# The entry of stage 3 begun ahead of the engines' meeting, with the gate row sent through DRAM and the backward states placed among the last taps

## The chip, the cores and the metric

The kernel runs on one core of one Trainium2 chip. The metric is the device time of one launch in microseconds; three runs of a kernel are taken and their median is compared. Beside them one execution is taken by the hardware profiler, and the rows below come from it. A core has TensorE (PE, with its weight loads PEld), VectorE (DVE), ScalarE (ACT), GpSimd (POOL) and SyncE (SP), which only issues DMAs here, and 16 DMA engines.

## What is computed

One inference step of a hybrid layer, for 256 context tokens and 2048 latent tokens of width 1024:

```
h   = rmsnorm(x) * (1 + scale1) + shift1
q,k,v,r,z,ga,gg = split(h @ w_in)
o   = gla_forward(q,k,v,g_f(z)) + gla_backward(q,k,v,g_b(z))   # chunks of 64, 4 heads
o   = rmsnorm_head(o) * silu(r)
u   = silu(layernorm(depthwise_conv31(ga * sigmoid(gg)) + b))
x   = x + gate1 * (concat(o, u) @ w_out)
h   = rmsnorm(x) * (1 + scale2) + shift2
x   = x + gate2 * expert_choice_moe(h)                         # 16 experts
y   = rmsnorm(x)
scale, shift, gate = silu(cond) @ w_mod + b_mod               # one set per request
```

The outputs are y of both token sets and the final forward and backward states of the context.

## The kernel before, in words

All matrices are kept in fp32; a product is made of three matmuls of split operands (a high and a low part, `three`, lines 1519 to 1521). The high part is a copy by ScalarE, the low part a subtraction on VectorE or GpSimd.

**Stage 2** goes over five blocks of tokens: the prompt (256 tokens), then latent blocks 0 to 3 (512 each), by `stage2(b, nb)` on every engine, b the block and nb the next one. TensorE projects the rows (`proj_half`, `proj_part`), makes the intra-chunk scores and outputs (`scores`, `outputs`), and in blocks 0 to 2 also two columns' worth of w_mod products, `mod_chunk(b, 0)` to `(b, 3)`, before and after `outputs(b, 3)`, which `mod_back` turns into columns and VectorE's `mod_tiles` writes into `mod`. w_mod reaches SBUF in two buffers (`raw`), by `load_mod(b, m)` on SyncE's queue; `load_mod(b, 2)` waits until `mod_chunk(b, 0)` has read its buffer. VectorE makes the depthwise convolution as 124 shifted multiply-adds (`taps(b, first, end)`, line 2258, the accumulator in `acc`), with the forward state recursion (`states`, line 2285) at fixed places between them. Results of a block are parked in DRAM: `park_q`, `park_o` (`store_o`), `park_r` (`store_r`), `park_s` (chunk states) and last `park_c` (the convolution), all by SyncE, in the written order of its `stage2`.

**The meeting.** `stage_end(eng, 1)` drains each engine and lets all wait for all. SyncE first waits until every store of the last block has landed (`stage2_done`). SBUF is laid out anew for stage 3: the weights of w_out (`wo_hl`), `cat` (the concatenation), `S3`, `q`, `r`, the staging buffers `wstage`, and `gt1` lie where stage 2 had its tiles.

**Stage 3** goes over m = 0 (the prompt) and m = 1 to 4 (latent blocks 3 down to 0). For each m the parked data are loaded (`load_c`, `load_qS`, `load_o`, `load_r`), the convolution's mean is taken on TensorE (`conv_mean`) and subtracted by VectorE (`centre`), the backward states are formed by VectorE (`back_states`, line 2305), their contribution is multiplied on TensorE (`inter`, line 1764) and added (`add_inter`), sums of squares (`sums`) give the norms (`stat_roots`, `stat_recips`, `stat_hi`, `spread`), and the output projection follows (`out_half`), a tile of 128 tokens at a time. `inter` has two banks: its third head waits until `add_inter` has taken the first.

Stage 3 begins with a `prologue` on TensorE, ScalarE and VectorE for m = 0, in which also w_out is split into parts (`wo_hi(k)` on ScalarE, `wo_lo(k)` on VectorE, in pairs k per staging buffer), the gate row gate1 is spread over all partitions into `gt1`, the router's weights are scaled (`wrA`), and the router's bias row is formed (`brow_of`). Before the change gt1 is made so: VectorE multiplies the identity by a column of `mod` into `diag`, TensorE multiplies ones by diag, ScalarE copies the four banks. Each engine works through its own instructions in the written order and waits on semaphores.

`mod_d` is a small DRAM tensor by which columns of `mod` are turned into rows: later in stage 3 (m = 2) four of its rows are stored, after it two more, each by a DMA of this form:

```
sp.dma_start(mod_d[i, cnd].rearrange("(k p) -> p k", p=128), cols[:, :, cnd],
             allow_slow_non_contiguous=True).then_inc(e_mod.sem, 16)
```

## Time and profile before

| | us |
|---|---|
| median of three runs | 2610.89 |
| lowest and highest | 2608.91, 2612.08 |
| the profiled execution, its own time | 2607.07 |
| its span, first to last instruction | 2605.0 |
| stage 2, last tap | 799.6 |
| first output matmul of stage 3 | 847.57 |

In the page of the profile TensorE is busy 2388.8 us (92%), VectorE 1653.4 (63%), ScalarE 1189.2 (46%), GpSimd 735.0 (28%). The time from some 1330 us on belongs to the experts. All times in rows are us from the start of the span, durations in a timeline are us; "mean ns" columns are marked as such. A timeline row merges neighbouring instructions of one line (x16 is sixteen of them), and in brackets stands how long the engine was idle before it and what released it. In a chain row stand the start, the time that the piece holds the chain, and the engine and line. The granted TensorE clock is given as a share of the full one, 1.00 or 0.50.

### The profile page before, as it was taken

How to read it: one execution, taken by the hardware profiler on the slowest of the kernel's cores; microseconds unless marked ns; L12 is line 12 of the kernel's file. 1: busy time of each engine (PE TensorE's matmuls, PEld its weight loads, DVE VectorE, ACT ScalarE, POOL GpSimd, SP SyncE). 2: the span in 40 equal slices, each digit the busy share in tenths (PEclk: the TensorE clock that was granted, in tenths of full speed). 3: DMA queues.
4: the chain of work that ended last, by engine and by line, in shares of the span. 5: the costliest groups of instructions: out<-in, count | busy, mean ns of one | idle time of the engine just before them, and what ended most of it. 6: DMA issues, size and time to landing. Idle time of an engine off the chain costs nothing.

```text
span 2605.0 us, 41287 instructions
## 1 busy us (share of the span) xinstructions
PE 2388.8 (92%) x15500; PEld 2138.2 (82%) x15500; DVE 1653.4 (63%) x2793; ACT 1189.2 (46%) x1916; POOL 735.0 (28%) x671
## 2 busy tenths in 40 slices
PE   5879999999995899996569999999999999999994
PEld 1868878787894577875169999999999999999994
DVE  1797969689597554523836656666665666666575
ACT  2646354453422333331145555445555545555563
POOL 1000000000000130110033445554445555444451
PEclk9989999999996899997579999999999999999997
DMA  7885575746536556524255667776667776666885
GB/s 242 322 305 193 175 252 182 262 164 227 189 127 207 166 161 143 166 96 128 70 151 185 180 199 199 199 212 191 188 182 205 199 206 196 188 187 196 280 253 193
DMA packets 287555, 505.73 MB, mean 194 GB/s; under 512 B 32094, under 2 KB 230587, under 8 KB 271578
## 3 DMA queue, kind: packets, MB, share of 16 engines
q1 hardware_dynamic: 248042, 377.93, 44.2%
q0 software_dynamic: 39408, 126.38, 18.7%
q8 instruction: 68, 1.11, 0.2%
q14 instruction: 37, 0.30, 0.0%
HBM read 405.73 MB, written 98.53 MB: 194 GB/s over the span
## 4 chain that ended last, share of the span: by engine, by line
PE 57%; DVE 5%; DMA 3%; ACT 2%; issue 1%; POOL 1%; SPq 0%; DVEq 0%; ACTq 0%; POOLq 0%
PE bank L1519 17%; PE bank L1521 17%; PE bank L1520 17%; PE bank L1764 1%; PE bank L1832 1%; DMA work_out<-park_s 1%; DVE work_exp L2511 1%; DMA out_dram<-work_exp 1%; PE bank L1780 1%; PE bank L1821 1%; DVE work_proj L2258 1%; PE bank L1783 1%; DVE work_out L2305 1%; PE bank L1772 1%; POOL x_rows L1458 0%
## 5 line engine op out<-in xcount | busy, mean ns | idle before, releaser
L1519 PE MATMUL bank<-act_hl_exp,hl_exp 128*128 128x288 f32 x3072 | 913.6, 297 | 37.2 <-POOL act_hl_exp L1437 24.0
L1520 PE MATMUL bank<-act_hl_exp,hl_exp 128*128 128x288 f32 x3072 | 910.2, 296 | 0.0
L1521 PE MATMUL bank<-act_hl_exp,hl_exp 128*128 128x288 f32 x3072 | 908.7, 296 | 0.0
L1519 PEld LDWEIGHTS bank<-act_hl_exp,hl_exp 128*128 128x128 f32 x3072 | 579.8, 189 | 40.6 <-issue 28.9
L1521 PEld LDWEIGHTS bank<-act_hl_exp,hl_exp 128*128 128x128 f32 x3072 | 581.8, 189 | 0.0
L1520 PEld LDWEIGHTS bank<-act_hl_exp,hl_exp 128*128 128x128 f32 x3072 | 580.6, 189 | 0.0
L2629 DVE TENSOR_TENSOR hl_exp<-work_exp,hl_exp 128x1024 fp32r<-128x1024 f32 x192 | 231.7, 1227 | 228.5 <-ACT hl_exp L1126 228.5
L2629 DVE TENSOR_TENSOR hl_exp<-raw_exp,hl_exp 128x1024 fp32r<-128x1024 f32 x192 | 232.2, 1225 | 200.5 <-ACT hl_exp L1126 200.5
L2258 DVE SCALAR_TENSOR_TENSOR work_proj<-work_proj,wcv 128x392 f32<-128x392 f32 (+11 forms) x600 | 337.0, 634 | 0.0
L1126 ACT ACTIVATE hl_exp<-work_exp 128x1024 fp32r<-128x1024 f32 x192 | 199.4, 1055 | 218.5 <-PE bank L1521 213.0
L1126 ACT ACTIVATE hl_exp<-raw_exp 128x1024 fp32r<-128x1024 f32 x192 | 198.5, 1052 | 166.5 <-PE bank L1521 166.4
L1437 POOL TENSOR_TENSOR act_hl_exp<-work_exp,act_hl_exp 128x288 fp32r<-128x288 f32 x128 | 156.3, 1239 | 386.9 <-ACT act_hl_exp L1149 386.9
L1458 POOL DMA_INDIRECT x_rows<-work_exp x135 | 242.9, 1799 | 61.6 <-issue 36.0
L1519 PE MATMUL bank<-act_hl_proj,hl_proj 128*128 128x512 f32 (+1 forms) x672 | 246.8, 367 | 5.8 <-DVE hl_proj L2105 4.2
L1521 PE MATMUL bank<-act_hl_proj,hl_proj 128*128 128x512 f32 (+1 forms) x672 | 242.7, 361 | 0.0
L1520 PE MATMUL bank<-act_hl_proj,hl_proj 128*128 128x512 f32 (+1 forms) x672 | 242.6, 361 | 0.0
L1307 POOL DMA_DIRECT2D hl_proj<-park_w x80 | 42.7, 535 | 645.1 <-PE bank L1521 565.8
L1424 POOL DMA_INDIRECT work_exp<-h_rows,work_exp x135 | 160.6, 1190 | 49.1 <-issue 36.6
L1142 ACT ACTIVATE work_exp<-work_exp 128x256 f32<-128x256 f32 (+1 forms) x256 | 109.4, 497 | 115.3 <-DVE work_exp L2639 67.0
L1519 PEld LDWEIGHTS bank<-act_hl_proj,hl_proj 128*128 128x128 f32 x672 | 128.7, 192 | 26.0 <-issue 5.5
L1521 PEld LDWEIGHTS bank<-act_hl_proj,hl_proj 128*128 128x128 f32 x672 | 128.2, 191 | 19.0
L1520 PEld LDWEIGHTS bank<-act_hl_proj,hl_proj 128*128 128x128 f32 x672 | 128.6, 191 | 17.5
(330 smaller groups left out, 3456.0 us busy)
## 6 DMA issues: line engine op xcount, KB each, us to landing
hl_proj<-park_w POOLq DMA_DIRECT2D x80, 1024.0 KB, 5.5
raw_exp<-in_w_e_gate_dram SPq DMA_DIRECT2D x32, 1024.0 KB, 5.7
raw_exp<-in_w_e_up_dram SPq DMA_DIRECT2D x32, 1024.0 KB, 5.7
work_exp<-in_w_e_gate_dram SPq DMA_DIRECT2D x32, 1024.0 KB
work_exp<-in_w_e_up_dram SPq DMA_DIRECT2D x32, 1024.0 KB, 6.4
raw_exp<-in_w_e_down_dram SPq DMA_DIRECT2D x32, 1024.0 KB, 5.5
work_exp<-in_w_e_down_dram SPq DMA_DIRECT2D x32, 1024.0 KB, 5.5
park_w<-hl_proj SPq DMA_DIRECT2D x10, 2048.0 KB, 11.8
```

The costliest lines, as they stand in the source:

```text
L1126: act.activation(half_out(j, q, 0), half_in(src, j, q), ACT.Copy).then_inc(s_hi, 1)
L1142: last = act.activation(h32e[:, k % 2, a:z], xT[:, k % 2, a:z], ACT.Identity, scale=A2q[:, cnd, k:k + 1], bias=sh2q[:, cnd, k:k + 1])
L1307: pool.dma_start(hl[:, j % 2, q], park_w[j, :, q]).then_inc(s_w[j % 2][q].sem, 16)
L1424: pool.indirect_dma_start(xg[:, b, :], None, h2_rows[:, :], bass.IndirectOffsetOnAxis(ap=ids_g[:, b:b + 1], axis=0)).then_inc(e_gat, 16)
L1437: pool.tensor_tensor(xe_hl[:, 1, k, :], h32e[:, k % 2, :], xe_hl[:, 0, k, :].bitcast(f32), ALU.subtract)\
L1458: pool.indirect_dma_start(x2_quarters[:, :], bass.IndirectOffsetOnAxis(ap=ids_s[:, b:b + 1], axis=0), y_t[:, b, :], None, compute_op=ALU.a ...
L1519: pe.matmul(out, lh, rh, start=first, stop=False)
L1520: pe.matmul(out, lh, rl, start=False, stop=False)
L1521: return pe.matmul(out, ll, rh, start=False, stop=last_)
L1764: last = pe.matmul(psum[7 - h % 2][:, 64 * cc:64 * cc + 64], S3[:, cc + 1, 128 * h:128 * h + 128], part("q", m, h)[:, 64 * cc:64 * cc + 64 ...
L2258: dve.scalar_tensor_tensor(out=ac[:, :, a0:a1], in0=uu[:, :, a0 + off:a1 + off], scalar=wcv[:, ct, w:w + 1], in1=ac[:, :, a0:a1], op0=ALU. ...
L2629: dve.tensor_tensor(half_out(j, q, 1), half_in(src, j, q), half_out(j, q, 0).bitcast(f32), ALU.subtract) .then_inc(s_lo[j % 2], 1)
```

## The change

Parts of stage 3's entry are moved ahead of the meeting. SyncE loads c, q, the states, o and r of m = 0 behind the last `store_o` of the last block; the first three loads of w_out are issued ahead of the drain, behind the landing of park_c. The gate row goes through DRAM: in block 1 (`b.i == 1`), behind `store_r(b, n, 3)` and ahead of `load_mod(b, 2)`, two DMAs store gate1's columns into a fourth row pair of `mod_d`, and behind the meeting two broadcast loads fill `gt1`; diag, its matmuls and the copies are gone, and the first residual waits for the loads. TensorE makes conv_mean(0) and both bias products at the end of its stage 2. VectorE puts `back_states(0, ...)` and `centre(0)` behind the fourth of the last twelve taps. In the prologues, ScalarE's head squares go ahead of wo_hi(2), and wrA goes behind wo_lo(3).

```diff
--- before.py
+++ after.py
@@ -124,7 +124,7 @@
         h2_rows = dram("h2_rows", (NTOK * NQ, HQ))
         h2_of = h2_rows.rearrange("(t q) c -> t q c", q=NQ)
         x2_quarters = x2_rows.rearrange("t (q c) -> (t q) c", q=NQ)
-        mod_d = dram("mod_d", (3, 2, D))
+        mod_d = dram("mod_d", (4, 2, D))
         park_q = dram("park_q", (1 + NBLK, 128, H, BT))
         park_o = dram("park_o", (1 + NBLK, 128, H, BT))
         park_r = dram("park_r", (1 + NBLK, 128, H, BT))
@@ -212,7 +212,6 @@
         selc = W3["selc"].rearrange("p (h c) -> p h c", h=5)
         spread_rs = reset.bitcast(f32r)[0:64, 0:BT]
         spread_sel = reset.bitcast(f32r)[0:64, BT:BT + 5]
-        diag = W3["sq"].rearrange("p (j c) -> p j c", j=16)
         wstage = [W3[n].rearrange("p (k c) -> p k c", k=2) for n in ("x", "xn", "h2")]
 
         def part(name, m, h):
@@ -339,7 +338,7 @@
 
         r_qS, r_o, r_r, r_c = sem("r_qS"), sem("r_o"), sem("r_r"), sem("r_c")
         r_wh, r_wl = sem("r_wh"), sem("r_wl")
-        r_sel, r_dg, r_gt, r_gr = sem("r_sel"), sem("r_dg"), sem("r_gt"), sem("r_gr")
+        r_sel, r_gst, r_gr = sem("r_sel"), sem("r_gst"), sem("r_gr")
         r_wr, r_br = sem("r_wr"), sem("r_br")
         r_c0, r_bs, r_c1, r_nst = sem("r_c0"), sem("r_bs"), sem("r_c1"), sem("r_nst")
         r_in, r_o1, r_sq, r_me, r_xc, r_csq = (sem("r_in"), sem("r_o1"), sem("r_sq"), sem("r_me"), sem("r_xc"),
@@ -541,11 +540,23 @@
                 store_o(b, n, 1 if b.prompt else 2)
                 store_r(b, n, 2)
                 store_r(b, n, 3)
+                if not b.prompt and b.i == 1:
+                    b.wait(sp, s_modv, 0)
+                    for cnd in range(2):
+                        sp.dma_start(mod_d[3, cnd].rearrange("(k p) -> p k", p=128), mod[:, 16:24, cnd],
+                                     allow_slow_non_contiguous=True).then_inc(r_gst, 16)
                 if not b.prompt:
                     if b.mod:
                         load_mod(b, 2)
                         load_mod(b, 3)
                     store_o(b, n, 3)
+                if nb is None:
+                    stage2_done(sp, Blk(b.i - 1))
+                    b.wait(sp, s_qst, 16)
+                    load_c(0)
+                    load_qS(0)
+                    load_o(0)
+                    load_r(0)
                 b.wait(sp, s_fs, b.NC)
                 b.wait(sp, s_ue, b.NC)
                 sp.dma_start(park_s[n, :, 0:b.NC, :], S_t[:, 0:b.NC, :]).then_inc(s_sst.sem, 16)
@@ -631,15 +642,14 @@
                 stage2(Blk(i), Blk(i + 1))
             stage2(final, None)
             stage2_done(sp, final)
+            final.wait(sp, s_c1, 1)
+            wo_v = w_out[0].rearrange("(j k p) c -> j p k c", p=128, k=2)
+            for i in range(3):
+                sp.dma_start(wstage[i], wo_v[i]).then_inc(r_wo[i].sem, 16)
             stage_end(sp, 1)
-            wo_v = w_out[0].rearrange("(j k p) c -> j p k c", p=128, k=2)
-            load_c(0)
-            load_qS(0)
-            load_o(0)
-            sp.dma_start(wstage[0], wo_v[0]).then_inc(r_wo[0].sem, 16)
-            load_r(0)
-            sp.dma_start(wstage[1], wo_v[1]).then_inc(r_wo[1].sem, 16)
-            sp.dma_start(wstage[2], wo_v[2]).then_inc(r_wo[2].sem, 16)
+            sp.wait_ge(r_gst, 32)
+            for cnd in range(2):
+                sp.dma_start(gt1[:, cnd, :], mod_d[3, cnd].partition_broadcast(128)).then_inc(r_gr, 16)
             sp.wait_ge(r_bs, NC3[0])
             sp.dma_start(new_bwd[0, 0].rearrange("h k v -> k h v"),
                          S3[64:128, 0, :].rearrange("k (h v) -> k h v", h=H)).then_inc(r_nst, 16)
@@ -975,8 +985,6 @@
                     act.wait_ge(r_xc, 4 * m + ct + 1)
                     if ct == 0:
                         wait_pos(act, r_st, m)
-                        if m == 0:
-                            act.wait_ge(r_gt, 4)
                     act.activation(part("sq", m, ct), cat_f(m)[:, 4 + ct, :], ACT.Square).then_inc(r_csq, 1)
 
             def head_squares(m, heads=range(H)):
@@ -1048,13 +1056,9 @@
                 conv_squares(0)
                 wo_hi(0)
                 wo_hi(1)
-                for j in range(4):
-                    act.wait_ge(r_gt, j + 1)
-                    act.activation(gt1[:, j // 2, 512 * (j % 2):512 * (j % 2) + 512], psum[j][:, :], ACT.Copy)\
-                       .then_inc(r_gr, 1)
+                head_squares(0)
                 wo_hi(2)
                 wo_hi(3)
-                head_squares(0)
                 wo_hi(4)
                 wo_hi(5)
                 stat_roots(0)
@@ -1692,6 +1696,12 @@
                     mod_chunk(b, 2)
                     mod_chunk(b, 3)
                     mod_back(b)
+                if nb is None:
+                    conv_mean(0)
+                    b.wait(pe, s_ue, b.NC)
+                    b.wait(pe, s_modv, 0)
+                    brow_of(0)
+                    brow_of(1).then_inc(r_br, 1)
 
             def mod_chunk(b, m):
 
@@ -1804,7 +1814,6 @@
                         wait_pos(pe, r_lg, g - 2 if late(g - 2) else g - 1)
                 elif q == 0:
                     pe.wait_ge(r_wl, KC)
-                    pe.wait_ge(r_gr, 4)
                 for k in range(KC):
                     if q == 0 and k % 4 == 0:
                         upto(pe, r_lo, piece(m, t, k // 4))
@@ -1833,26 +1842,16 @@
                                      stop=(k == KC - 1))
                 last.then_inc(r_ro, 1)
 
+            def brow_of(c):
+                for k in range(KC):
+                    last = pe.matmul(psum[5][:, NE * c:NE * c + NE], mod[:, 24 + k, c:c + 1].broadcast_to([128, 128]),
+                                     wr[:, k, :], start=(k == 0), stop=(k == KC - 1))
+                return last
+
             def prologue():
-                def brow_of(c):
-                    for k in range(KC):
-                        last = pe.matmul(psum[5][:, NE * c:NE * c + NE],
-                                         mod[:, 24 + k, c:c + 1].broadcast_to([128, 128]), wr[:, k, :],
-                                         start=(k == 0), stop=(k == KC - 1))
-                    return last
-
-                conv_mean(0)
-                for j in range(16):
-                    pe.wait_ge(r_dg, j + 1)
-                    last = pe.matmul(psum[j // 4][:, 128 * (j % 4):128 * (j % 4) + 128], ones[:, :], diag[:, j, :],
-                                     start=True, stop=True)
-                    if j % 4 == 3:
-                        last.then_inc(r_gt, 1)
                 inter(0)
-                brow_of(0)
                 pe.wait_ge(r_sel, 7)
                 sums(0)
-                brow_of(1).then_inc(r_br, 1)
                 spread(0)
                 pe.wait_ge(r_wr, 2)
 
@@ -2228,7 +2227,11 @@
                     lo_rows(nb, 3)
                 taps(b, 106, 112)
                 states(b, 3)
-                taps(b, 112, TAPS)
+                taps(b, 112, 116)
+                if nb is None:
+                    back_states(0, 0, NC3[0])
+                    centre(0)
+                taps(b, 116, TAPS)
 
             def glu(b, ct):
                 b.wait(dve, s_sg, ct + 1)
@@ -2361,6 +2364,8 @@
                 for q in range(2):
                     upto(dve, r_T, 2 * g + q + 1)
                     if q == 0:
+                        if g == 0:
+                            dve.wait_ge(r_gr, 32)
                         upto(dve, r_x[g % 2], 16 * (g // 2 + 1))
                         wait_pos(dve, r_h2st[g % 2], 16 * (g // 2))
                         if g >= 2:
@@ -2382,25 +2387,20 @@
 
             def prologue():
                 dve.tensor_tensor(spread_sel, ident[0:64, 0:5], ident[0:64, 32:37], ALU.add)
-                for j in range(16):
-                    dve.tensor_scalar(diag[:, j, :], ident[:, :], mod[:, 16 + j % 8, j // 8:j // 8 + 1], None, ALU.mult)\
-                       .then_inc(r_dg, 1)
-                for c in range(2):
-                    dve.tensor_tensor(wrA[:, c], wr[:, :, :], A2[:, :, c:c + 1].broadcast_to([128, KC, NE]),
-                                      ALU.mult).then_inc(r_wr, 1)
 
                 def wo_lo(k):
                     dve.wait_ge(r_wh, k + 1)
                     dve.tensor_tensor(wo_hl[:, 1, k, :], wstage[k // 2 % 3][:, k % 2, :], wo_hl[:, 0, k, :].bitcast(f32),
                                       ALU.subtract).then_inc(r_wl, 1)
 
-                centre(0)
-                back_states(0, 0, NC3[0])
                 wo_lo(0)
                 wo_lo(1)
                 add_inter(0)
                 wo_lo(2)
                 wo_lo(3)
+                for c in range(2):
+                    dve.tensor_tensor(wrA[:, c], wr[:, :, :], A2[:, :, c:c + 1].broadcast_to([128, KC, NE]),
+                                      ALU.mult).then_inc(r_wr, 1)
                 gate_heads(0)
                 wo_lo(4)
                 wo_lo(5)
```

## Rows read from the trace of the kernel before

**Rows 1.** Windows: busy us per engine, clock, DMA share; a middle block; one later slice

```profile
340.00:497.00 157.00, 155.88 (x920) 127.80 (x919) 125.20 (x198) 74.80 (x119) 10.81 (x20) 1.00 0.64 214
852.00:853.00 1.00, 1.00 (x4) 0.81 (x3) 0.00 (x0) 0.00 (x0) 1.00 (x2) 0.58 0.88 295
```

**Rows 2.** Chain of waits over the passage, 799 to 848 us

```profile
799.61 3.83 DMA park_c<-work_proj
...
805.62 10.40 DMA work_out<-park_s
...
821.58 7.06 PE bank L1764 x32
828.64 3.33 PE bank L1839 x16
...
847.57 0.77 PE bank L1519
```

**Rows 3.** Timeline of SyncE's queue, the passage

```profile
789.00 0.53 SPq L511 DMA_DIRECT2D park_o<-work_proj  x1
...
803.66 0.58 SPq L584 DMA_DIRECT2D work_out<-park_c  x1
```

**Rows 4.** Timeline of VectorE, the passage

```profile
792.80 6.77 DVE L2258 SCALAR_TENSOR_TENSOR work_proj<-work_proj,wcv 128x432 f32<-128x432 f32 x12
...
807.38 0.48 DVE L2389 TENSOR_TENSOR work_out<-wr,A 128x128 f32<-128x128 f32 x2
811.53 1.42 DVE L2321 SCALAR_TENSOR_TENSOR work_out<-bank,work_out 128x256 f32<-128x256 f32 x4 [3.66 <-PE bank L1772]
...
816.69 4.74 DVE L2305 SCALAR_TENSOR_TENSOR work_out<-work_out,dec 64x128 f32<-64x128 f32 x16
...
829.01 2.35 DVE L2394 TENSOR_TENSOR wo_hl<-work_out,wo_hl 128x1024 fp32r<-128x1024 f32 x2
831.28 1.43 DVE L2336 TENSOR_TENSOR work_out<-work_out 128x256 f32<-128x256 f32 x4
...
837.95 1.74 DVE L2341 RECIPROCAL work_out<-work_out 5x256 f32<-5x256 f32 x1 [2.97 <-ACT work_out L992]
```

**Rows 5.** Timeline of ScalarE, the passage

```profile
819.93 2.00 ACT L1046 ACTIVATE wo_hl<-work_out 128x1024 fp32r<-128x1024 f32 x2 [3.17 <-DMA work_out<-in_w_out_dram]
...
828.73 1.34 ACT L987 ACTIVATE work_out<-work_out 128x256 f32<-128x256 f32 x4 [2.77 <-PE bank L1764]
```

**Rows 6.** Timeline of SyncE's queue, end of block 1

```profile
466.71 10.23 SPq L506 DMA_DIRECT2D park_r<-work_proj  x2
477.65 3.84 SPq L502 DMA_DIRECT2D raw_proj<-in_w_mod_dram  x2
```

**Rows 7.** Timeline of TensorE, block 1 and the end of block 3

```profile
484.15 7.07 PE L1702 MATMUL bank<-raw_proj,scond 128*2 128x256 f32 x32 [0.35 <-DMA raw_proj<-in_w_mod_dram]
...
786.53 1.16 PE L1748 MATMUL bank<-work_proj 128*128 128x128 f32 x8
```

**Rows 8.** DMA issues: count, KB each, median us to landing; 837 to 853.5 us

```profile
work_out<-park_q SPq DMA_DIRECT2D x1, 1024.0 KB, 5.5
```

**Rows 9.** SyncE's queue around 1003; landings of L616, that store's and all

```profile
1003.14 1.06 SPq L661 DMA_DIRECT2D mod_d<-A  x2
1004.25 2.84 SPq L661 DMA_DIRECT2D mod_d<-mod  x2
1014.18 0.33 SPq L616 DMA_DIRECT2D x_rows<-work_out  x1
...
DMA to landing us min/median/max: 10.3/10.3/10.3
...
DMA to landing us min/median/max: 2.6/2.7/17.3
```

**Rows 10.** Timeline of SyncE's queue around 1297

```profile
1297.63 1.00 SPq L703 DMA_DIRECT2D mod_d<-mod  x2
1301.08 0.56 SPq L682 DMA_DIRECT2D raw_exp<-in_w_e_gate_dram  x1
```

**Rows 11.** DMA issues, 1297 to 1312 us

```profile
raw_exp<-in_w_e_gate_dram SPq DMA_DIRECT2D x1, 1024.0 KB, 16.4
```

## The prediction

> **What bounds the kernel now.** I read the table of windows first. In a middle block of stage 2 TensorE is busy 155.88 of 157 us and VectorE 125.20 [rows 1]: until the last block ends, whatever makes TensorE late is paid in full, and there is no slack behind in which to make it up. Then comes the chain of waits over the passage from stage 2 to stage 3 [rows 2]. The last tap ends at 799.6, the store of park_c takes 3.83 us, the engines meet, the loads go out, the later half of the states lands at 805.62 + 10.40 = 816.02, the backward states run until 821.4, inter(0) takes 7.06 us at the low clock, the first bias product 3.33, then come the sums, the roots, the reciprocal at 837.95, and the first output matmul at 847.57. That is 48 us with TensorE mostly idle or waiting, and it is what the change attacks. The timeline of SyncE's own queue comes third [rows 3], because the change issues DMAs in three places of it, one of them two blocks earlier.
>
> **Entry loads and VectorE.** The six loads for m = 0 go out behind the last store_o, issued at 789.00 [rows 3], so from about 789.9. Before, the first was issued at 803.66 [rows 3] and the states were there at 816.02 [rows 2], 12.4 us later, with 0.5 MB each of c, q and twice S ahead and w_out interleaved behind. The new order has the same 2 MB ahead and park_s (2 MB) behind in place of w_out, so I keep 12.4 us: the states land at 802.3. The inserted work stands behind tap 115. States(3) end at 792.8, twelve taps take 6.77 [rows 4], 0.56 each, so tap 115 ends at 795.1 and VectorE then waits 7.2 us for the load, with eight taps queued behind the wait, and behind those the park_c store and the meeting. Backward states with their memset: 816.02 to 821.44, 5.4 us [rows 2] (16 products 4.74 [rows 4]) until 807.7. Centring 1.42 [rows 4] until 809.1 (its conv_mean runs on an idle TensorE). Eight taps, 4.5, until 813.6. park_c 3.83 [rows 2] until 817.4. So VectorE leaves stage 2 14 us later than before, and 5.4 + 1.4 of that is work that only changed sides; the rest is the wait.
>
> **Behind the meeting.** The first w_out pair needs SBUF that park_c's source holds, so it is issued at 817.6. A 1 MB load with others close behind it landed in 5.5 us (park_q, [rows 8]), so call T = 823.1 the time that w_out's first pair is there. inter(0) begins at the meeting, near 818, but its third head needs the bank that add_inter frees, and add_inter stands behind wo_lo(0) and wo_lo(1), so T sets the pace. Two wo_hi of 1.0 [rows 5], one wo_lo of 1.2 [rows 4], one addition (about 0.4, estimated from the centring's 1.42 for four of that size), two heads of inter at 7.06/4 each [rows 2]: T + 7.1 = 830.2. Head squares 1.34 [rows 5]: 831.5, and only then wo_hi(2) and (3), 2.0, for which wo_lo(3) waits: 834.7. wrA 0.48 for both, gate_heads 1.43, wo_lo(4) and (5) 2.35 [rows 4]: the reciprocal starts at 839.0, before at 837.95 [rows 4]. From there the chain to the first output matmul is unchanged (9.6 us). Balance of the passage: **+1 us**. What is taken out there buys nothing: diag (VectorE waits afterwards anyway), the gate matmuls and the four copies of gt1, and brow 3.33 on the chain [rows 2], whose time is given back because the wo_hi/wo_lo pairs, formerly done before TensorE got there, now start at T. Moved into TensorE's idle end of stage 2, conv_mean and both brows cost nothing; without that cover they would cost about 3.5 us each. The two gt1 broadcasts have until the first residual, tens of us. Bounds: if the states arrive at 798 (2 MB at nearly the full rate), 4.3 us less, -3.3 in all; if w_out's first pair shares the queue evenly with the second and third and needs 10 us, +5.5. How much longer than an instant the drain takes with loads under way no row shows; a meeting as late as the end of the w_out loads lies inside the upper bound. I take +1.
>
> **The gate row's way out, in block 1.** Each of the two stores to mod_d writes 1024 elements of 4 bytes, one per packet. They are issued behind store_r(3), that is at 466.71 + 10.23 = 476.9, and straight behind them load_mod(2), before issued at 477.65 [rows 6]. It landed at 484.15, which is where TensorE began mod_chunk(2), having waited 0.35 us for that very DMA [rows 7]: no slack at all. What do such stores do to the queue? The trace has them twice, same shape and same queue. Four of them went out from 1003.14; the x2_rows store issued at 1014.18 landed after 10.3 us [rows 9], against 2.7 as the median of that line [rows 9], so the queue was blocked until about 1021.8, 18.7 us for four, 9.3 for two. Two of them went out at 1297.63, and the weight load issued at 1301.08 [rows 10] landed 16.4 us later [rows 11], 19.9 us after the first store (here gathers shared the engines). Carried to block 1: by the first, 476.9 + 9.3 + 6.5 (the load's own 477.65 to 484.15) = 492.7, TensorE late by 8.6; by the second, 476.9 + 19.9 = 496.8, late by 12.7. I take 10.5, between them, a little nearer the one without gathers. load_mod(3), the park_o and park_s stores and the x tiles follow in the queue; none is due sooner than the delay allows. The array goes cold in such a wait: after the idle passage the dense output matmuls started at 847.57 [rows 2] and ran at the low clock until the slice 852 to 853, where the grant is 0.58 in the mean [rows 1]; 5 us at half speed cost 2.5. Together **+13 us**, and since TensorE is the bound there [rows 1], all of it reaches the end.
>
> The queue model behind this has a page. The trace shows a read delayed by stores that stand ahead of it in the same queue [rows 9, 11]. "DMA: Bandwidth & Descriptors" of the Trainium skill, section Queues, rings and completion order, says that on each DMA engine a ring's descriptors are consumed in order, and its Rules for kernel authors that a strided last dimension becomes one descriptor per element; so far the trace agrees. But the same page, section Two DMAs through the same engine are not ordered, says that descriptors are pipelined and a later one need not wait for an earlier one's write. By that alone the load would go once the small packets are read; the rows say longer. It is rival A, priced below from rows.
>
> **Sum.** 13 + 1 = +14 us. The profiled execution took 2607.07 us (span 2605.0), 3.8 below the median of the three runs: 2621 in an execution like it, 2625 as the median. Own range 2618 (8.6 + 2 of block 1, -3.3 of the passage) to 2632 (12.7 + 2.5 and +5.5).
>
> **Rivals.**
> A. The load passes the stores' slow writes and is late only by half of the smaller figure, 4.3 us, too short for the clock to fall far. For it: in block 1 nobody needs the stores' landing. Against: the 10.3 and 16.4 us. 4.3 + 1 gives 2616.
> B. The stores are hidden altogether: the queue takes them while load_mod(2) is still waiting for mod_chunk(0), and nothing is late. Then only +1 is left, 2612, no measurable change; the change then moves work that was hidden, and its saving is nil. Against it: 0.35 us of wait shows no slack.
> C. Faster: the states land before tap 115 ends, since nothing but park_o is under way at 789.9. The 7.2 us wait vanishes: passage 1 - 7.2 = -6.2, 2605 if block 1 loses nothing. It is a gain that a measurement can tell only if the states land by 796 (6 us after issue, half of what the trace shows) and block 1 is late by less than 1 us. This is what the change would give if the early loads were as free as they look.
>
> **How the numbers follow.** Forecast 0.52, A 0.14, B 0.22, C 0.12. About 0.2% (5 us) is what a measurement can tell from no change. Slower by more: the forecast and most of A, 0.63. Within: B and the rest of A, 0.25. Faster: 0.12. The range runs from 2608 (B with the passage at its lower bound) to 2632; C and the tails are left out, under 2 in 10.
>
> **What would show it.** In block 1 a wait of 8 to 13 us of TensorE for the DMA of w_mod into raw_proj, with the grant at 0.5 behind it, and every later block shifted by 11 to 15 us. In VectorE's last block a wait of about 7 us for park_s after the fourth of the last twelve taps. The meeting some 14 us later against the end of TensorE's stage 2; ACT's first wo_hi some 5 us behind the meeting; the time from TensorE's last product of stage 2 to the first output matmul 60 to 61 us, as before (786.53 + 1.16 = 787.7 [rows 7] to 847.6). The forecast is wrong if the w_mod load lands in its usual 6.5 us, or if that last stretch shrinks by more than 4 us.

## The result and the profile after

The changed kernel takes 2621.9 us, the median of five runs (2620.7 to 2627.6), against 2610.9 for the kernel before (2608.5 to 2612.1): ratio 1.0053, 95% interval [1.0042, 1.0065]. It is slower; the medians differ by 11.0 us, the ratio stands for 13.8 (0.0053 x 2610.9), the forecast was +14. The profiled execution took 2623.2 us, its span is 2621.5.

Block 1 first. SyncE's queue in the changed kernel, start and duration in us, answers to [rows 6]:

```profile
474.34 0.32 SPq L505 DMA_DIRECT2D park_r<-work_proj  x1
474.71 1.45 SPq L546 DMA_DIRECT2D mod_d<-mod  x2
476.20 3.16 SPq L501 DMA_DIRECT2D raw_proj<-in_w_mod_dram  x2
482.83 5.83 SPq L510 DMA_DIRECT2D park_o<-work_proj  x1
```

TensorE in the same block answers to [rows 7]:

```profile
471.72 7.07 PE L1712 MATMUL bank<-raw_proj,scond 128*2 128x256 f32 x32
...
492.17 8.72 PE L1712 MATMUL bank<-raw_proj,scond 128*2 128x256 f32 x32 [10.66 <-DMA raw_proj<-in_w_mod_dram]
```

The same 32 products waited 0.35 us for this DMA before [rows 7] and wait 10.66 now; they take 8.72 instead of 7.07, since the first of them run at the low clock. Together +12.0 us in one place. The windows show the wait from the side of the DMA engines (columns as in [rows 1]: TensorE's busy time first, and last the clock, the DMA engines' busy share, GB/s):

```profile
474.00:482.00 8.00, 7.52 (x47) 4.19 (x44) 8.00 (x13) 2.94 (x6) 0.00 (x0) 1.00 0.74 154
482.00:486.00 4.00, 0.00 (x0) 0.00 (x0) 3.87 (x12) 0.80 (x2) 0.00 (x0) 0.92 0.83 39
486.00:488.00 2.00, 0.00 (x0) 0.00 (x0) 2.00 (x4) 0.00 (x0) 0.00 (x0) 0.50 0.79 39
488.00:490.00 2.00, 0.00 (x0) 0.00 (x0) 2.00 (x5) 0.00 (x0) 0.00 (x0) 0.50 0.72 205
490.00:492.00 2.00, 0.00 (x0) 0.00 (x0) 1.29 (x3) 0.00 (x0) 0.00 (x0) 0.50 1.06 363
492.00:496.00 4.00, 3.83 (x11) 1.17 (x12) 0.00 (x0) 0.00 (x0) 0.00 (x0) 0.55 1.15 406
496.00:500.00 4.00, 4.00 (x20) 1.61 (x19) 0.00 (x0) 0.00 (x0) 0.00 (x0) 1.00 0.96 408
```

From 482 to 488 the DMA engines are four fifths busy and move 39 GB/s; ten microseconds later, at a share of 0.96, they move 408. What they are busy with shows in the packets on record, from 476 to 482 and from 482 to 488:

```profile
DMA packets 2291, 0.63 MB, mean 105 GB/s; under 512 B 2112, under 2 KB 2120, under 8 KB 2248
...
DMA packets 230, 0.24 MB, mean 39 GB/s; under 512 B 0, under 2 KB 230, under 8 KB 230
```

The 4-byte pieces pass in the first six microseconds. In the second six none of them is on record, and the 230 packets have 1 KB each, the size in which w_mod is read: the loads are under way, at a tenth of their later rate. The two stores land only some 12 us after their issue, at about 487, and from 488 on the rate comes back:

```profile
mod_d<-mod SPq DMA_DIRECT2D x2, 4.0 KB, 12.0
```

By this trace the loads pay for the time until the stores have landed, and not only for that in which the pieces go out. TensorE's clock falls to 0.50 (1.2 GHz) in the idle stretch and is back at 1.00 (2.4 GHz) from 496 on.

Then the passage: the chain of waits of the changed kernel, start, time held, engine and line; it answers to [rows 2].

```profile
801.54 10.64 DMA work_out<-park_s
...
823.60 3.83 DMA park_c<-work_proj
827.55 5.02 DMA work_out<-in_w_out_dram
832.59 1.06 ACT wo_hl L1054
...
836.43 3.69 PE bank L1774 x16
840.20 1.33 ACT work_out L995 x4
...
848.89 1.66 DVE work_out L2344
...
858.42 0.77 PE bank L1523
```

VectorE's timeline there answers to [rows 4]:

```profile
802.53 2.38 DVE L2261 SCALAR_TENSOR_TENSOR work_proj<-work_proj,wcv 128x432 f32<-128x432 f32 x4
812.34 0.48 DVE L2300 MEMSET work_out<- 64x512 f32 x1 [7.44 <-DMA work_out<-park_s]
812.86 4.73 DVE L2308 SCALAR_TENSOR_TENSOR work_out<-work_out,dec 64x128 f32<-64x128 f32 x16
...
819.09 4.48 DVE L2261 SCALAR_TENSOR_TENSOR work_proj<-work_proj,wcv 128x416 f32<-128x416 f32 x8
```

VectorE now stands for 7.44 us in front of the states, with eight taps, the store of park_c and the meeting behind it; then the chain runs the same links as before, in another order. The last product of stage 2 is

```profile
796.26 1.16 PE L1758 MATMUL bank<-work_proj 128*128 128x128 f32 x8
```

and ends at 797.42. From there to the first output matmul at 858.42 it is 61.0 us, before 847.57 - 787.69 = 59.9 [rows 2, 7]. So the passage, rebuilt from end to end, is 1.1 us longer than it was, in this pair of executions. That is no more than it varies by itself: in the eight kernels below whose stage 3 is that of before (e2, e3, e5, e6, e9 to e12) it took 59.0 to 61.6 us. What is shown is that it got no shorter.

The two places give 12.0 + 1.1 = 13.1 us. The spans of the profiled executions differ by more, 16.5, because single executions scatter: up to block 1 the changed one was 2.3 us ahead (471.72 against 474.00 at the first w_mod product), and behind the first output matmul it took 2621.5 - 858.4 = 1763.1 us against 1757.4. In the profiles of the six kernels below that have before's stage 3 and ran on chips as fast as these (e2, e3, e5, e6, e11, e12) that rest was 1758.6 to 1766.0. The 1763.1 lies inside, the 1757.4 just below, so no effect of the change shows there.

### The profile page after: what moved, and what is told of

Read it like the earlier page. It is cut to its first block, busy times and chain, and to the rows that moved or that the text cites. A ratio compares the mean times of both kernels' runs of the same rounds, so it can differ in the third digit from the quotient of the medians.

```text
span 2621.5 us, 41212 instructions
## 1 busy us (share of the span) xinstructions
PE 2389.6 (91%) x15468; PEld 2137.2 (82%) x15468; DVE 1651.7 (63%) x2777; ACT 1187.1 (45%) x1912; POOL 734.9 (28%) x671
## 4 chain that ended last, share of the span: by engine, by line
PE 79%; DVE 5%; DMA 5%; ACT 2%; issue 1%; POOL 1%; SPq 1%; ACTq 0%; DVEq 0%; POOLq 0%
PE bank L1523 23%; PE bank L1525 22%; PE bank L1524 22%; PE bank L1774 1%; PE bank L1841 1%; PE bank L1712 1%; DMA raw_proj<-in_w_mod_dram 1%; PE bank L1739 1%; DMA work_out<-park_s 1%; DVE work_exp L2511 1%; PE bank L1751 1%; DMA out_dram<-work_exp 1%; PE bank L1830 1%; PE bank L1758 1%; DVE work_out L2308 1%
## 5 line engine op out<-in xcount | busy, mean ns | idle before, releaser
L1462 POOL DMA_INDIRECT x_rows<-work_exp x135 | 242.8, 1798 | 61.6 <-issue 36.0
```

Source lines behind the costliest of these rows:

```text
L1462: pool.indirect_dma_start(x2_quarters[:, :], bass.IndirectOffsetOnAxis(ap=ids_s[:, b:b + 1], axis=0), y_t[:, b, :], None, compute_op=ALU.a ...
```

## The experiments

In "before plus ..." the kernel before is kept and only the two stores (or a form of them) are put into block 1, into DRAM that nobody reads later; `mod_d` is made larger for them, and SyncE waits for their landing ahead of the meeting. A wait of TensorE is read from one profiled execution per kernel; the same two stores gave 10.66 us in the changed kernel and 9.72 in e2, so differences of 1 us between waits mean nothing. Each comes with runs of before on the same chip; times are compared only there.

### Which of the two places costs the time

**e1_stores_elsewhere**: the whole change, with the two stores moved from block 1 to block 2, behind the store of park_q.

```diff
+                if not b.prompt and b.i == 2:
+                    b.wait(sp, s_modv, 0)
+                    for cnd in range(2):
+                        sp.dma_start(mod_d[3, cnd].rearrange("(k p) -> p k", p=128), mod[:, 16:24, cnd],
+                                     allow_slow_non_contiguous=True).then_inc(r_gst, 16)
                 for j in range(7, NPROJ):
...
                 store_r(b, n, 3)
-                if not b.prompt and b.i == 1:
...
```

> The changed kernel with one edit: the two stores of the gate columns go out in block 2 behind the store of park_q, where the queue has nothing to issue for some 37 us, and not in block 1 ahead of a w_mod load. Queue theory (the small stores hold up the load behind them, TensorE waits 10.7 us for it and then runs 1.65 us longer at the low clock): the wait in block 1 is 0.4 us again, the kernel is about 12 us faster than the changed one, 2610, level with the kernel before within 3 us. Rival (the loss is in the passage to stage 3, the wait of block 1 would be made up later): no change, 2620 to 2622.

Measured: 2608.9 us, before 2609.4, ratio 0.9996 [0.9987, 1.0005]. The same products in block 1:

```profile
483.09 7.07 PE L1712 MATMUL bank<-raw_proj,scond 128*2 128x256 f32 x32 [0.42 <-DMA raw_proj<-in_w_mod_dram]
```

The wait is gone and so is the whole loss. The passage is still 61.2 us long (787.22 to 848.37). At their new place the stores cost nothing that shows: SyncE issues no other DMA for 34 us behind them, and the longest wait of TensorE for a DMA in the rest of that block is 0.7 us.

**e2_stores_alone**: before plus the two stores as the change has them.

```diff
                 store_r(b, n, 3)
+                if not b.prompt and b.i == 1:
+                    b.wait(sp, s_modv, 0)
+                    for cnd in range(2):
+                        sp.dma_start(mod_d[3, cnd].rearrange("(k p) -> p k", p=128), mod[:, 16:24, cnd],
+                                     allow_slow_non_contiguous=True).then_inc(r_gst, 16)
```

> The kernel before with one addition: the same two stores at the place that the change gave them (block 1, ahead of the w_mod load), read by nobody. Queue theory: TensorE waits 10 to 11 us in block 1, the kernel is 11 to 13 us slower than before, 2622 to 2624. Rival (the loss is in the passage): 2611, no change.

Measured: 2620.8 us, before 2609.4, ratio 1.0043 [1.0031, 1.0055], which is +11.2:

```profile
492.14 9.23 PE L1709 MATMUL bank<-raw_proj,scond 128*2 128x256 f32 x32 [9.72 <-DMA raw_proj<-in_w_mod_dram]
```

Two DMAs of 4 KB each, whose result nobody uses, make up the loss. The wait and the time lie a little under what I had expected (10 to 11, 2622). The two runs close the account: the stores cost about 11 us, and all the rest of the change together (e1) nothing that can be told from zero, -3.4 to +1.3 by the interval.

### What it is in the stores

**e3_contiguous_store**: before plus one store of the same 8 KB, left in the order in which it lies in SBUF, so 128 pieces of 64 bytes.

```diff
+                if not b.prompt and b.i == 1:
...
+                    sp.dma_start(mod_d[3].rearrange("c (p e) -> (c p) e", e=16), mod[:, 16:24, :].rearrange("p k c -> p (k c)")).then_inc(r_gst, 16)
```

> The kernel before with the same 8 KB stored at that same place, but in 128 pieces of 64 bytes by one DMA and not in 2048 pieces of 4 bytes by two; read by nobody. If the number of small writes is what holds the queue up: a wait under 1.5 us in block 1 and a time within 2 us of before, 2610 to 2613. If any store to DRAM at that place delays the load by the time of its landing: a wait of some 3 us or more in block 1, 2614 or more. If even 64-byte pieces are as slow as 4-byte ones in sum: 2621 or more.

Measured: 2609.4 us, ratio 1.0001 [0.9993, 1.0010].

```profile
483.58 7.07 PE L1707 MATMUL bank<-raw_proj,scond 128*2 128x256 f32 x32 [0.22 <-DMA raw_proj<-in_w_mod_dram]
```

The same bytes at the same place cost nothing that shows. This is no finished cure: in this order they aren't the row that the broadcast loads read, and no run tested the re-ordering.

**e6_four_stores**: e2 with four such stores instead of two.

```diff
-                    for cnd in range(2):
+                    for r_, cnd in ((3, 0), (3, 1), (4, 0), (4, 1)):
-                        sp.dma_start(mod_d[3, cnd].rearrange("(k p) -> p k", p=128), mod[:, 16:24, cnd],
+                        sp.dma_start(mod_d[r_, cnd].rearrange("(k p) -> p k", p=128), mod[:, 16:24, cnd],
```

> The kernel before with four stores of 4-byte pieces (16 KB in all) and not two, at the place of the change in block 1; read by nobody. If each store adds its own time to the queue (18.7 us for four in the trace of before, so about 4.7 each): a wait of 18 to 20 us in block 1, 2629 to 2632. If most of the two stores' delay is a fixed price of one slow write at the end: a wait of 11 to 13 us, 2621 to 2624.

Measured: 2628.3 us, before 2609.5, ratio 1.0070 [1.0055, 1.0085].

```profile
498.48 8.48 PE L1709 MATMUL bank<-raw_proj,scond 128*2 128x256 f32 x32 [18.03 <-DMA raw_proj<-in_w_mod_dram]
```

Four stores, 18.0 us of wait; two, 9.7. The price of such stores adds up, 4.2 us for each one more; the 18.7 that [rows 9] give for four lie near.

**e9_pieces_apart**: e2 with the same 1024 pieces of 4 bytes in each store, each piece 512 bytes from the next in DRAM.

```diff
+        mod_w = dram("mod_w", (2, D, 128))
...
-                        sp.dma_start(mod_d[3, cnd].rearrange("(k p) -> p k", p=128), mod[:, 16:24, cnd],
+                        sp.dma_start(mod_w[cnd].rearrange("(k p) e -> p k e", p=128)[:, :, 0], mod[:, 16:24, cnd],
```

> The kernel before with the two stores of 1024 pieces of 4 bytes at the place of the change in block 1, but into a DRAM tensor in which the pieces lie 512 bytes apart and not side by side; read by nobody. The pieces, their number and their source are the same. If the price is the number of small pieces: a wait of TensorE of 9 to 12 us for the w_mod load, 2619 to 2623, as with the stores alone (9.7 us, 2620.8). If it is that pieces written side by side by different DMA engines collide in one stretch of DRAM: a wait under 3 us, 2609 to 2612.

Measured: 2636.2 us, before on this chip 2628.4, ratio 1.0033 [1.0022, 1.0044]. (This chip is the slower one for both kernels, and the surplus lies in the experts' part: 1777.7 us behind the first output matmul.) TensorE's wait is 4.64 us:

```profile
486.55 8.41 PE L1710 MATMUL bank<-raw_proj,scond 128*2 128x256 f32 x32 [4.64 <-DMA raw_proj<-in_w_mod_dram]
```

Neither expectation holds: 4.6 us is between the two. About half of the 9.7 us of e2 thus goes with the pieces' lying side by side and not with their count and size. This rests on the waits of two profiled executions, on two chips; in total time the intervals of e2 and e9 overlap.

**e11_wide_pieces_apart** and **e12_wide_pieces_adjacent**: again two stores of 1024 pieces, but each piece 64 bytes wide (data of `wr`), in e11 (below) 512 bytes apart, in e12, where `mod_w` is (2, D, 16), side by side.

```diff
+        mod_w = dram("mod_w", (2, D, 128))
...
+                        sp.dma_start(mod_w[cnd].rearrange("(k p) e -> p k e", p=128)[:, :, 0:NE], wr[:, :, :],
```

> Before with two stores at the change's place in block 1, each of 1024 pieces as in the change, but each piece 64 bytes (16 elements of the router's weights) and the pieces 512 bytes apart in DRAM, into a tensor that nobody reads. Same count of pieces and same spacing as the run with 4-byte pieces apart, where TensorE waited 4.6 us. If it is the count of pieces that holds the DMA engines, the wait stays at 4 to 6 us and the kernel is some 8 us above before. If it is the write of less than 64 bytes, the wait falls to 2 us or less and the time is within 3 us of before.

> The same stores of 1024 pieces of 64 bytes each, with the pieces side by side in DRAM. By the count of pieces alone: as the 4-byte stores side by side, where TensorE waited 9.7 us, or at least as the pieces apart (4 to 6 us). If several pieces that share 64 bytes of memory are what made the stores of the change dear, these, which share none, cost no more than the pieces apart: a wait under 5 us. If short writes as such are the price, a wait of 2 us or less.

Measured: 2612.5 us, ratio 1.0014 [1.0003, 1.0025], and 2613.9 us, ratio 1.0013 [1.0001, 1.0026], before 2609.6. The wait is the same in both:

```profile
483.68 7.07 PE L1710 MATMUL bank<-raw_proj,scond 128*2 128x256 f32 x32 [2.13 <-DMA raw_proj<-in_w_mod_dram]
```

```profile
484.72 7.07 PE L1710 MATMUL bank<-raw_proj,scond 128*2 128x256 f32 x32 [2.13 <-DMA raw_proj<-in_w_mod_dram]
```

Sixteen times the bytes, a fifth of the wait. With 64-byte pieces the distance makes no difference that shows; with 4-byte pieces it halves the wait. As an estimate from single waits, that of e2 falls into about 2.1 us for 2048 pieces as such (e3, with 128, has 0.2), 2.5 for their being 4 bytes and not 64 (4.64 - 2.13), and 5.1 for several of them falling next to each other (9.72 - 4.64). That the last is several short writes to one small stretch of memory, taken one after another, is my reading of it and not shown: no run varied the distance between 4 and 512 bytes, so how far apart is far enough stays open.

### Is it the place in the queue

**e5_stores_by_act**: before plus the two stores issued from ScalarE's queue, behind its `gate(b, 3)`, instead of ahead of the loads in SyncE's.

```diff
                 gate(b, 3)
+                if not b.prompt and b.i == 1:
+                    b.wait(act, s_modv, 0)
+                    for cnd in range(2):
+                        act.dma_start(mod_d[3, cnd].rearrange("(k p) -> p k", p=128), mod[:, 16:24, cnd],
+                                      allow_slow_non_contiguous=True).then_inc(r_gst, 16)
```

> The kernel before with the two 4-byte-piece stores added at the same moment of block 1, but issued from ScalarE's own queue behind the block's last gate, so that they stand in another ring than the w_mod load; read by nobody. If what holds the load up is its place behind the stores in one ring: TensorE's wait in block 1 stays under 3 us, the kernel within 3 us of before, 2609 to 2612. If the small writes block the DMA engines themselves, whatever the ring: a wait of 7 us or more, 2616 to 2621, as with the stores alone on SyncE's queue (9.7 us, 2620.8).

Measured: 2629.3 us, before 2609.5, ratio 1.0071 [1.0059, 1.0084]: worse than in SyncE's queue. ScalarE's queue and TensorE:

```profile
473.67 1.03 ACTq L912 DMA_DIRECT2D mod_d<-mod  x2
```

```profile
500.35 9.00 PE L1709 MATMUL bank<-raw_proj,scond 128*2 128x256 f32 x32 [17.17 <-DMA raw_proj<-in_w_mod_dram]
```

And the landings in that stretch (KB each, median us from issue to landing):

```profile
raw_proj<-in_w_mod_dram SPq DMA_DIRECT2D x2, 1024.0 KB, 23.0
park_r<-work_proj SPq DMA_DIRECT2D x1, 256.0 KB, 21.5
park_o<-work_proj SPq DMA_DIRECT2D x1, 256.0 KB, 17.3
```

In the changed kernel park_r, issued just ahead of the stores in the same queue, landed after 7.5 us and the w_mod loads behind them after 16.6. Here the stores go out first, and every transfer takes turns with them: from 476 to 485, 25 packets of GpSimd's loads are on record and 22 of the stores. And where e2 has one slow stretch, there are two (the last number of a row is GB/s):

```profile
476.00:485.00 9.00, 7.18 (x45) 4.07 (x43) 8.87 (x16) 3.44 (x6) 0.00 (x0) 1.00 0.61 23
485.00:488.00 3.00, 0.00 (x0) 0.00 (x0) 3.00 (x8) 0.00 (x0) 0.00 (x0) 0.87 0.94 275
488.00:492.00 4.00, 0.00 (x0) 0.00 (x0) 4.00 (x9) 0.00 (x0) 0.00 (x0) 0.50 1.16 49
492.00:496.00 4.00, 0.00 (x0) 0.00 (x0) 0.94 (x3) 0.00 (x0) 0.00 (x0) 0.50 1.17 111
```

About half of the pieces pass by 476, most of the others from 487 on, and each half is followed by its own slow stretch. Which of the two matters, the other queue or the earlier moment (the stores stand 2.3 us ahead of park_r here, and behind it in e2), this run doesn't separate. The taking of turns agrees with the Trainium skill, "DMA: Bandwidth & Descriptors", section Issuing engines are not separate DMA queues, by which DMAs of all issuing engines end up on the same 16 engines and interleave.

**e10_behind_last_load**: e2 with the stores behind `load_mod(b, 3)`, the last load that is due in the block.

```diff
                         load_mod(b, 3)
+                        if not b.prompt and b.i == 1:
+                            b.wait(sp, s_modv, 0)
+                            for cnd in range(2):
...
                     store_o(b, n, 3)
```

> The kernel before with the same two stores as in the second experiment (side by side in DRAM), but two lines later in block 1: behind load_mod(3) and not ahead of load_mod(2). Theory (the small writes stop whatever is under way on the DMA engines for some 10 us, and it costs only what is due in that time): load_mod(2) has landed, load_mod(3) is under way, the park_o and x loads have slack, so TensorE waits at most 3 us, the kernel is within 3 us of before, 2609 to 2612. Rival (load_mod(3), issued just ahead of the stores, is held up like the load behind them was): a wait of 5 us or more, 2616 or more.

Measured: 2635.8 us, before 2628.4 (the chip of e9), ratio 1.0023 [1.0008, 1.0038]. TensorE:

```profile
482.30 3.62 PE L1709 MATMUL bank<-raw_proj,scond 128*2 128x256 f32 x16 [0.22 <-DMA raw_proj<-in_w_mod_dram]
490.25 4.97 PE L1709 MATMUL bank<-raw_proj,scond 128*2 128x256 f32 x16 [4.33 <-DMA raw_proj<-in_w_mod_dram]
```

The first load keeps its time, the second, though issued ahead of the stores, comes 4.3 us late. This lies between the two expectations for the wait (3 and 5 us), and the total is 7 us above before, so the rival was nearer. Standing ahead in the queue helps and doesn't protect.

### What the passage could give

**e4_states_behind_taps**: e1 with backward states and centring behind the last tap and the carry copy.

```diff
+                if nb is None:
+                    back_states(0, 0, NC3[0])
+                    centre(0)
...
-                taps(b, 112, 116)
-                if nb is None:
-                    back_states(0, 0, NC3[0])
-                    centre(0)
-                taps(b, 116, TAPS)
+                taps(b, 112, TAPS)
```

> As the first of this call (stores in block 2), and besides the backward states and the centring of m = 0 go behind the last tap and the copy of the carry, still ahead of the meeting. No computation is left out. Theory (in the changed kernel VectorE's wait of 7.4 us for the states and 7 us of stage 3 work stand ahead of the last eight taps, and so of the park_c store and of the w_out loads that pace the prologue): the last tap ends 12 to 14 us earlier against TensorE's end of stage 2, w_out is there some 10 us earlier, and the kernel is 9 to 12 us faster than the first of this call, about 2600. Rival (the meeting waits for VectorE in either order, so the passage is as long): within 2 us of the first of this call.

Measured: 2604.3 us, before 2609.4, ratio 0.9978 [0.9968, 0.9989]; passage 55.0 us, 6.2 less than e1's, and the median 4.6 below e1's, where I had expected 9 to 12. The last tap ends 14.4 us earlier against the end of TensorE's stage 2, as expected. The chain says what took the rest:

```profile
798.29 12.18 DMA park_c<-work_proj
...
810.59 4.95 DMA work_out<-in_w_out_dram
```

The store of park_c, 3.83 us long in [rows 2] and in the changed kernel, takes 12.18 when it is issued at 798.3: by their landings park_s (2 MB, until 808.0) and the last 1.5 MB of the entry loads (until 803.1) are still under way. The wait for the states had covered that; without it the store pays.

**e7_o_r_late**: e4 with `load_o` behind the store of park_c and `load_r` behind the second load of w_out.

```diff
                     load_qS(0)
-                    load_o(0)
-                    load_r(0)
...
             stage2(final, None)
+            load_o(0)
...
+                if i == 1:
+                    load_r(0)
```

> The kernel of the fourth experiment (stores in block 2, states behind the taps) with one edit: of the early loads only c, q and the states stay ahead of the park_s store; o goes behind the park_c store, r behind the second w_out load. Theory (there the park_c store took 12.2 us and not 3.8 because 3 MB of loads and 2 MB of park_s stood ahead of it): park_c lands 2 to 4 us earlier, the kernel is 2 to 4 us faster than that one, 2600 to 2602. Rival (the time is set by the drain of all of it, in whatever order): no change, 2604.

Measured: 2602.9 us, before 2609.5, ratio 0.9971 [0.9960, 0.9982]. The store of park_c takes 8.72 us, and the passage is 51.5, 3.5 shorter, as expected; in the total that gain can't be told from e4's, whose interval overlaps.

**e8_inter_first**: e7 with `add_inter(0)` ahead of the first two wo_lo, and wo_hi(2) ahead of the head squares.

```diff
-                head_squares(0)
                 wo_hi(2)
+                head_squares(0)
...
+                add_inter(0)
                 wo_lo(0)
                 wo_lo(1)
-                add_inter(0)
```

> As the one above, and in the prologue VectorE adds inter's result before its first two wo_lo, and ScalarE makes the third wo_hi ahead of the head squares, so that inter(0) no longer waits for w_out. Theory (T, the landing of w_out's first pair, paces inter's third head through add_inter's place): inter(0) runs through without its gap of 3.5 us, the reciprocal comes 3 to 6 us earlier against T, the kernel is 3 to 5 us faster than the one above, 2596 to 2598. Rival (VectorE's eight wo_lo after T set the end in any order): within 1.5 us of it.

Measured: 2598.4 us, before 2609.5, ratio 0.9959 [0.9946, 0.9971]. Its chain:

```profile
799.63 8.86 DMA park_c<-work_proj
...
811.07 7.10 PE bank L1775 x32
818.20 0.42 DVE work_out L2332
...
836.71 0.77 PE bank L1524
```

All 32 products of inter run in one piece at the meeting, while w_out is still on its way, instead of half of them behind the additions. The passage is 49.0 us (787.7 to 836.7), 2.5 shorter than e7's, a little less than the 3 to 5 expected, and the intervals of the two totals overlap. Against before the passage is 10.9 us shorter and the medians differ by 11.1, so this version beats both kernels. The longest piece left on its chain is the store of park_c, 8.9 us.

## Why the prediction was right, and where it wasn't

**Block 1.** Forecast: late by 10.5 (between 8.6 and 12.7), cold clock 2.5. Measured: 10.66 - 0.35 = 10.3, and 8.72 - 7.07 = 1.65. Of the two carried prices that of [rows 9], which made TensorE late by 8.6, was the nearer; e2, with the stores alone, is late by 9.4 (9.72 - 0.35). That 10.3 came out next to my 10.5 is in part luck, as the same stores vary by 1 us between these two kernels. The clock's term was too large because I took 5 us at half speed for it; 1.65 lost is 3.3 us at half speed, and the windows have the clock at 1.00 from 496 on, 3.8 us after the products begin. In e2 the same term is 2.16 (9.23 - 7.07). 12.0 for 13.

**The mechanism of block 1** was right in its half that counts, the price of the pieces (e3, e6), and wrong in its other half. I wrote that the load stands behind the stores in the same queue and that the queue is blocked (with [rows 9] as a read delayed, where it is a store; the delayed read is that of [rows 11]). e5 takes the stores out of that queue and the wait grows to 17.2; e10 puts them behind the load in it and 4.3 remain. What is held up is all that the DMA engines move, in whatever queue, and the loads' own packets crawl (39 GB/s) until the stores have landed. Whether the engines or the memory behind them set that rate no run separates; that the pieces' spacing in DRAM counts (e9) points to the memory, and stays an argument. By my model e5 would have been a cure, and the number for the change itself came out right because in its order the two models say the same. Rival A (late by 4.3, 2616) and B (hidden, 2612) are out: the wait is 10.66. The rule behind A, in the Trainium skill, "DMA: Bandwidth & Descriptors", section Two DMAs through the same engine are not ordered, that a later descriptor need not wait for an earlier one's write, isn't refuted: 230 packets of the loads pass from 482 to 488, before the stores have landed. It gives little relief here, since they pass at a tenth of the later rate.

**Entry loads and VectorE.** States forecast 12.4 us after the first load, they came after 12.6 (799.57, the first load's issue, to 812.2); VectorE's wait forecast 7.2, measured 7.44. Rival C, states there before tap 115, is out.

**Behind the meeting.** From the last product of stage 2 to the issue of w_out forecast 29.9 us (787.7 to 817.6), measured 30.1 (797.42 to 827.55); T forecast 5.5 behind the issue, measured 5.0; reciprocal forecast T + 16, measured 848.89 - 832.57 = 16.3; the last stretch 9.6, measured 9.5. Sum +1 forecast, +1.1 measured. The links came out as forecast, each within 1 us; that the sum meets to 0.1 is luck, since the stretch varies from 59.0 to 61.6 us where nothing in it was changed. VectorE's last tap ends 14.3 us later against TensorE's last product of stage 2 than before, for 14 forecast. One item stood elsewhere than I put it: wo_hi starts 3.4 us behind the meeting (829.2), not 5, as the meeting comes 1.6 behind the issue of w_out.

**Where the gain went.** The change takes bias products, gate matmuls, copies and the entry loads out of a 48 us stretch and saves nothing: the 7.4 us wait inside the taps delays the meeting by as much as the earlier loads bring (e4 gets 6.2 us of it back by moving the inserted work), and two 4 KB stores 300 us earlier cost 12. The sum of 14 lies in the interval of the ratio, 11.0 to 17.0; the median that it gave, 2625, is 3 us above the measured 2621.9.

## What to carry to other kernels

Price a DMA by the number, size and spacing of its pieces, not by its bytes: 2048 pieces of 4 bytes side by side held up everything for 10 us, 2048 of 64 bytes for 2, and the same 8 KB in 128 pieces of 64 bytes cost nothing that shows. Neither another engine's queue (17.2 us) nor a place behind the urgent load (4.3) hides it; put such a store where no load is due for that long (e1), or find a layout with longer pieces. Work that waits for a load belongs behind all that doesn't, above all on an engine whose end releases a meeting. And when a wait is taken out, look up which transfer it had given a quiet time: here the next link tripled.

## What the runs showed of the hardware that I had not expected

- The stores issued from ScalarE's queue made TensorE wait 17.2 us, from SyncE's own 9.7, with the same pieces.
- 4-byte pieces side by side cost twice those 512 bytes apart (9.7 and 4.6 us), 64-byte pieces 2.1 at either distance (one profiled execution each).
- The 4-byte pieces were on record within some 5 us of their issue, but for as long as the stores hadn't landed, 12 us, the 1 KB packets of the loads behind them moved at 39 GB/s and not at 350 or more.
- The 1 MB store of park_c took 3.8 us with nothing else under way, 12.2 with park_s and the last 1.5 MB of the entry loads still under way (e4), and 8.7 and 8.9 with o and r, 1 MB, issued behind it (e7, e8).
